# Slots of odd experts on other partitions, expert rows stored by token, and the last norm's weights spread by TensorE

## The reference, cut to what matters

```python
logits = h @ w_router + b_router                 # 320 x 32
top_v, top_e = lax.top_k(logits, 4)              # four of 32 experts for each token
gate = softmax(top_v)
# for each chosen expert e of a token:
gu = xe @ w_gu[e] + b_gu[e]                      # 1024 x 2048, 8 MB of weights
gt, up = split(gu, 2)                            # clamped to 7
act = gt * sigmoid(1.702 * gt) * (up + 1.0)
out = act @ w_dn[e] + b_dn[e]                    # 1024 x 1024, 4 MB of weights
y[token] += gate * out
x = x + y
y_prompt, y_sample = rmsnorm(x, norm_final)      # for the 256 and the 64 tokens
```

## Time and profile before

| what | us |
|---|---|
| median of 3 runs | 1360.23 |
| lowest and highest | 1358.46, 1360.65 |
| the profiled execution's own time | 1357.94 |
| its span, first to last instruction | 1356.2 |
| TensorE busy | 1264.1 (93%) |
| VectorE busy | 459.0 (34%) |
| ScalarE busy | 230.7 (17%) |
| GpSimd busy | 123.2 (9%) |

### The profile page before, as it was taken

The page is one execution under the profiler, slowest core; times in us unless marked ns, Lnnn a source line. Parts: engine busy times, 40 slices in busy tenths (PEclk is TensorE's granted clock), DMA queues, the critical chain, the costliest instruction groups (busy, mean ns, idle before and its releaser), DMA issues.

```text
span 1356.2 us, 14399 instructions
## 1 busy us (share of the span) xinstructions
PE 1264.1 (93%) x5895; PEld 570.1 (42%) x5895; DVE 459.0 (34%) x809; ACT 230.7 (17%) x333; POOL 123.2 (9%) x164
## 2 busy tenths in 40 slices
PE   7999999999999999999999999999987778878786
PEld 5756766666543333333333333333322223222231
DVE  2897322211463322223113313222422222233226
ACT  4102432310221111111011111111211111111121
POOL 3110100000010100000000000100010000000020
PEclk9999999999999999999999999999999999999898
DMA  9715826465699999999999999999999999999994
GB/s 331 258 63 157 266 76 156 155 248 204 254 364 426 425 426 426 426 425 427 426 425 427 427 427 424 425 427 425 424 427 425 425 427 425 425 426 426 424 388 153
DMA packets 97115, 479.33 MB, mean 353 GB/s; under 512 B 43962, under 2 KB 46026, under 8 KB 72311
## 3 DMA queue, kind: packets, MB, share of 16 engines
q1 hardware_dynamic: 84641, 459.36, 83.3%
q0 software_dynamic: 11008, 15.63, 3.3%
q10 hardware_dynamic: 1374, 3.02, 0.6%
HBM read 477.57 MB, written 22.61 MB: 369 GB/s over the span
## 4 chain that ended last, share of the span: by engine, by line
PE 74%; DMA 23%; issue 1%; DVE 1%; ACT 0%; DVEq 0%; ACTq 0%
PE PS L1762 29%; PE PS L1400 15%; PE PS L1795 14%; DMA ring<-in_w_dn 12%; DMA ring<-in_w_gu 11%; PE PS L1340 4%; PE PS L1580 4%; PE PS L1624 3%; PE PS L1436 2%; PE PS L1847 1%; PE PS L1667 0%; PE PS L1527 0%; DMA XX<-in_x_prompt 0%; PE PS L1546 0%; PE PS L1644 0%
## 5 line engine op out<-in xcount | busy, mean ns | idle before, releaser
L1762 PE MATMUL PS<-ring,arena 128*64 128x512 f32 x1824 | 405.7, 597 | 39.2 <-DMA ring<-in_w_gu 27.6
L1251 DVE TENSOR_TENSOR arena<-PS,XX 128x1024 f32<-128x1024 f32 x32 | 39.2, 1224 | 659.2 <-PE PS L1762 659.2
L1762 PEld LDWEIGHTS PS<-ring,arena 128*64 128x64 f32 x1824 | 129.2, 139 | 293.7 <-issue 291.1
L1795 PE MATMUL PS<-ring,arena 128*64 128x512 f32 x896 | 203.7, 604 | 16.9 <-DMA ring<-in_w_dn 15.6
L1400 PE MATMUL PS<-arena,ring 128*128 128x320 f32 x768 | 213.5, 434 | 0.1
L1400 PEld LDWEIGHTS PS<-arena,ring 128*128 128x128 f32 x768 | 144.3, 190 | 58.7 <-issue 2.0
L1762 PE MATMUL PS<-arena 128*64 128x512 f32 x608 | 136.3, 595 | 11.6 <-DMA arena<-in_w_gu 10.8
L854 ACT ACTIVATE arena<-arena 128x1024 f32<-128x1024 f32 x32 | 33.9, 1058 | 618.4 <-DVE arena L1254 618.4
L554 POOL DMA_INDIRECT y_rows<-arena x60 | 59.8, 996 | 791.7 <-ACT arena L835 762.9
L1795 PEld LDWEIGHTS PS<-ring,arena 128*64 128x64 f32 x896 | 62.0, 139 | 142.0 <-issue 142.0
L1340 PEld LDWEIGHTS PS<-ident,arena 128*128 128x128 f32 (+3 forms) x580 | 63.1, 142 | 54.8 <-issue 49.0
(11 more groups left out here) (216 smaller groups left out, 670.2 us busy)
## 6 DMA issues: line engine op xcount, KB each, us to landing
ring<-in_w_gu SPq DMA_DIRECT2D x96, 2048.0 KB, 27.9
ring<-in_w_dn SPq DMA_DIRECT2D x48, 2048.0 KB, 29.3
arena<-in_w_gu SPq DMA_DIRECT2D x31, 2048.0 KB, 28.7
arena<-in_w_dn SPq DMA_DIRECT2D x16, 2048.0 KB, 30.0
ring<-in_w_in SPq DMA_DIRECT2D x11, 2048.0 KB, 11.3
ring<-in_w_mem_kv SPq DMA_DIRECT2D x2, 2048.0 KB, 20.7
ring<-in_cache_mem_k SPq DMA_DIRECT2D x32, 128.0 KB, 3.3
ring<-in_cache_mem_v SPq DMA_DIRECT2D x4, 1024.0 KB, 6.1
```

The source lines that it names most:

```text
L1251: nc.vector.tensor_tensor(gbuf[:], PS[:, 0:2, :], g_bias, ALU.add).then_inc(main["g_added"], 1)
L1762: last = mm(PS[64 * h:64 * h + 64, 2 * g + b, :], in_block(xT[:, k, :], b), (spare[kk] if m == BONUS else moe_ring(m, 2)[:, kk]) [:, g * D ...
L1795: last = mm(PS[64 * h:64 * h + 64, 4 + b, :], actT[:, b, j, c * BLK:(c + 1) * BLK], moe_ring(m, 4)[:, j, h * 512:(h + 1) * 512], start=c = ...
```

## The change

- **Slots.** A second table `iota_o` is made in which bit 4 of the slot is turned round (a6 xor a5 becomes its opposite). The gathered and scattered rows of odd experts lie by it, those of even experts by `iota_s`. In `listing`, three more small instructions per tile flip bit 4 of the slot number where the expert is odd, so that the one comparison with `iota_s` still serves. `hot_weights` takes `iota_o` for expert 31.
- **Rows by token.** Rank r of token t is now row `4 t + r`. All of `y_rows` is zeroed, not half. `rank_rows(tt)` loads all four ranks of one tile of tokens, as two transfers of two ranks each: pieces of 8 KB. Three places instead of four are used, and GpSimd waits for expert 29's scatters before the first of them.
- **Sum by tile.** DVE adds the four ranks of tile 0, then those of tile 1, then those of tile 2.
- **Last norm.** ACT loads the norm's weights early as two rows of 2 KB; TensorE spreads them over the partitions by two products with a row of ones, behind its last `to_tokens`, into PSUM banks 4 and 5, and DVE reads them there. The load of 512 KB at the end is gone.
- **TensorE's order at the end.** `bias_sum(2)` and `to_tokens(0, 0)` stand ahead of `down(31)`, `to_tokens(0, 1)` and `(0, 2)` between its two chunks.

```diff
-RANK_PLACES = [PLACE[-10], PLACE[-9], PLACE[-6], PLACE[-5]]
+RANK_PLACES = [PLACE[-10], PLACE[-9], PLACE[-6]]
...
-                sp.dma_start(y_rows[2 * T:4 * T, :].rearrange("(p j) c -> p (j c)", p=P).rearrange("p (n c) -> p n c", c=512),
-                             W[0].rearrange("p b t -> p (b t)")[:, None, 0:512].to_broadcast([P, 10, 512])) \
+                sp.dma_start(y_rows.rearrange("(p j) c -> p (j c)", p=P).rearrange("p (n c) -> p n c", c=512),
+                             W[0].rearrange("p b t -> p (b t)")[:, None, 0:512].to_broadcast([P, 20, 512])) \
...
-        sp.wait_ge(main["dn_done"], NE - 2)
-        sp.dma_start(normfin, a["norm_final"].partition_broadcast(P)).then_inc(fin_in, 16)
...
-        nc.gpsimd.iota(worth[:, :, :, 1], [[2 * P, TT], [-2 * T, TOPK]], base=2 * T * (TOPK - 1) - SKIP,
-                       channel_multiplier=2, allow_small_or_imprecise_dtypes=True).then_inc(consts, 1)
+        nc.gpsimd.iota(worth[:, :, :, 1], [[2 * TOPK * P, TT], [-2, TOPK]], base=2 * (TOPK - 1) - SKIP,
+                       channel_multiplier=2 * TOPK, allow_small_or_imprecise_dtypes=True).then_inc(consts, 1)
...
+                    columns = iota_o[:, 64 * a6 + 32 * a5:64 * a6 + 32 * a5 + 32] \
+                        .rearrange("p (c d e f b) -> p b c d e f", c=2, d=2, e=2, f=2)[:, odd]
+                    nc.gpsimd.iota(columns, [[2, 2], [1, 2], [8, 2], [32, 2]],
+                                   base=4 * a6 + 16 * (1 - (a6 ^ a5)) + BLK * odd,
...
-        def rank_rows(r):
-            nc.gpsimd.dma_start(yr(r)[:, 0:2, :], y_rows[r * T:r * T + 2 * P, :].rearrange("(t p) d -> p t d", p=P)) \
-                .then_inc(yr_in[r], 16)
-            nc.gpsimd.dma_start(yr(r)[0:ROWS[2], 2, :], y_rows[r * T + 2 * P:(r + 1) * T, :]).then_inc(yr_in[r], 16)
+        def rank_rows(tt):
+            r = ROWS[tt]
+            for j in range(0, TOPK, 2):
+                nc.gpsimd.dma_start(yr(tt)[0:r, j:j + 2, :], y_tokens[tt * P:tt * P + r, j:j + 2, :]).then_inc(yr_in[tt], 16)
...
-        pool.wait_ge(main["scattered"], 32 * (DIRECT[0] - 1))
+        pool.wait_ge(main["scattered"], 32 * DIRECT[0])
         rank_rows(0)
-        pool.wait_ge(main["scattered"], 32 * DIRECT[0])
         rank_rows(1)
         pool.wait_ge(main[consumed(RINGED[-6])[0]], consumed(RINGED[-6])[2])
         rank_rows(2)
-        pool.wait_ge(main["gu_done"], NE)
-        rank_rows(3)
...
+            act.dma_start(nrow[64 + 32 * h:65 + 32 * h, :], a["norm_final"][512 * h:512 * (h + 1)][None, :]).then_inc(fin_in, 16)
...
+            link(nc.vector.tensor_scalar(turn[0:r, tt, :], R8i[0:r, tt, :], 512, None, ALU.bitwise_and))
+            link(nc.vector.tensor_scalar(turn[0:r, tt, :], turn[0:r, tt, :], 16 / 512, None, ALU.mult))
             link(nc.vector.tensor_scalar(lowi[0:r, tt, :], R8i[0:r, tt, :], 511, None, ALU.bitwise_and))
+            link(nc.vector.tensor_tensor(lowi[0:r, tt, :], lowi[0:r, tt, :], turn[0:r, tt, :], ALU.bitwise_xor))
...
-            dve.wait_ge(summed, (TOPK - 1) * TT + tt + 1)
+            dve.wait_ge(summed, TOPK * (tt + 1))
...
-        for r in range(TOPK):
-            j = TOPK - 1 - r
-            dve.wait_ge(yr_in[r], 32)
-            for tt in range(TT):
-                n = ROWS[tt]
+        for tt in range(TT):
+            n = ROWS[tt]
+            dve.wait_ge(yr_in[tt], 32)
+            for r in range(TOPK):
+                j = TOPK - 1 - r
...
-        dve.wait_ge(fin_in, 16)
+        dve.wait_ge(norm_spread, 1)
...
         def amid_last():
-            bias_sum(2, False)
-            to_tokens(0, 0)
+            to_tokens(0, 1)
+            to_tokens(0, 2)
...
             pe.wait_ge(main["actT_ready"], NE)
+            bias_sum(2, False)
             pe.wait_ge(main["zs_ready"], NE - 1)
+            to_tokens(0, 0)
             down(0, e, amid_last)
-            to_tokens(0, 1)
-            to_tokens(0, 2)
...
+            spread_norm()
+
+        def spread_norm():
+            pe.wait_ge(fin_in, 32)
+            for h in range(2):
+                last = mm(PS[:, 4 + h, :], ones[64 + 32 * h:65 + 32 * h, :], nrow[64 + 32 * h:65 + 32 * h, :],
+                          start=True, stop=True)
+            last.then_inc(norm_spread, 1)
```

More of the change, by code:

```diff
@@ L222, in program @@
     iota_s = sb("iota_s", [P, WIN])
+    iota_o = sb("iota_o", [P, WIN])
+    turn = sb("turn", [P, TT, 8], I32)
     worth = sb("worth", [P, TT, TOPK, 2])
@@ L281, in program @@
         sem(s) for s in ("bdn_in", "dense_ready", "gt_done", "gt_ready", "bd_done", "bd_added"))
-    yr_in = [sem(f"yr_in{i}") for i in range(TOPK)]
-    fin_in, fin_out = sem("fin_in"), sem("fin_out")
+    yr_in = [sem(f"yr_in{tt}") for tt in range(TT)]
+    fin_in, fin_out, norm_spread = sem("fin_in"), sem("fin_out"), sem("norm_spread")
     zeroed, hot_made, w_turned, w_copied = sem("zeroed"), sem("hot_made"), sem("w_turned"), sem("w_copied")
@@ L296, in program @@
     y_rows = nc.dram_tensor("y_rows", (TOPK * T, D), F32, kind="Internal").ap()
+    y_tokens = y_rows.rearrange("(t r) d -> t r d", r=TOPK)
     y_half = y_rows.rearrange("r (h c) -> (r h) c", h=2)
@@ L334, in moe_loaded, with yr @@
         return loaded[s] if s < SLOTS else low_in[s - SLOTS]
-    def yr(r):
-        return room(RANK_PLACES[r]).rearrange("p (t n) -> p t n", t=4)[:, 0:TT, :]
-    normfin = room(RANK_PLACES[0]).rearrange("p (t n) -> p t n", t=4)[:, TT, :]
+    def yr(tt):
+        return room(RANK_PLACES[tt]).rearrange("p (r n) -> p r n", r=TOPK)
+    nrow = XN[:, 1, 512:D]
+    normfin = PS[:, 4:6, :].rearrange("p a b -> p (a b)")
     block = ctx.enter_context(nc.Block())
@@ L504, in _ @@
                     nc.gpsimd.iota(columns, [[2, 2], [1, 2], [8, 2], [32, 2]], base=4 * a6 + 16 * (a6 ^ a5) + BLK * odd,
+                                   channel_multiplier=0, allow_small_or_imprecise_dtypes=True)
+                    columns = iota_o[:, 64 * a6 + 32 * a5:64 * a6 + 32 * a5 + 32] \
+                        .rearrange("p (c d e f b) -> p b c d e f", c=2, d=2, e=2, f=2)[:, odd]
+                    nc.gpsimd.iota(columns, [[2, 2], [1, 2], [8, 2], [32, 2]],
+                                   base=4 * a6 + 16 * (1 - (a6 ^ a5)) + BLK * odd,
                                    channel_multiplier=0, allow_small_or_imprecise_dtypes=True)
@@ L1233, in hot_weights @@
                 r = ROWS[tt]
-                link(nc.vector.tensor_scalar(hotw[x][0:r, tt, :], iota_s[0:r, :], 1024.0 + 512.0 * e, R[0:r, tt, e:e + 1],
+                link(nc.vector.tensor_scalar(hotw[x][0:r, tt, :], (iota_o if e % 2 else iota_s)[0:r, :], 1024.0 + 512.0 * e, R[0:r, tt, e:e + 1],
                                              ALU.add, ALU.is_equal))
@@ L1312, in _ @@
         dve.nop()
-        for r in range(TOPK):
-            j = TOPK - 1 - r
-            dve.wait_ge(yr_in[r], 32)
-            for tt in range(TT):
-                n = ROWS[tt]
+        for tt in range(TT):
[3 more added lines that the diff above has]
+                j = TOPK - 1 - r
                 if r:
-                    dve.wait_ge(summed, (r - 1) * TT + tt + 1)
-                nc.vector.scalar_tensor_tensor(X[0:n, tt, :], yr(r)[0:n, tt, :], gates[0:n, tt, j:j + 1], X[0:n, tt, :],
+                    dve.wait_ge(summed, TOPK * tt + r)
+                nc.vector.scalar_tensor_tensor(X[0:n, tt, :], yr(tt)[0:n, r, :], gates[0:n, tt, j:j + 1], X[0:n, tt, :],
                                                ALU.mult, ALU.add).then_inc(summed, 1)
@@ L1940, in _ @@
                 over_window(2)
+                pe.wait_ge(main["zs_ready"], 3 * NE)
                 pe.nop()
@@ L1943, in _ @@
                 bias_sum(tt, True).then_inc(bd_done, 1)
+            pe.wait_ge(main["zs_ready"], 2 * NE)
+            spread_norm()
             pe.nop()
```

## The result

The changed kernel takes 1362.4 us (median; 1358.6 to 1364.8) where the kernel before took 1358.4 beside it; the ratio is 1.0021, 95% interval 1.0014 to 1.0028, or 2.9 us more. (The two medians lie 4.0 us apart, because the times of the kernel before fall into two groups, one near 1358 and one near 1360, and a median jumps between them; the ratio with its interval is the safer figure.) In the profiled executions the span is 1359.6 us against 1356.2. The forecast was 3.4 us less. The changed time lies above its range, on the side of rival 2. That rival 2 named 1362.6 is in part chance: it counted +2.4 us from a median of 1360.23, and beside the changed kernel that median was 1358.4.

The account below looks back on a forecast made before the run. DMA bytes bound the expert stage, the slowest engine the end. Balance 4.0, norm 1.2 and pieces 1.5 us land the last rows at 1333.8; after the tile sums -3.4 us remains: 1356.8 from median 1360.23, range 1355.1 to 1358.3.

Parts of the forecast that it names:

- rival 2: At the end, turning bit 4 does nothing and eight sums follow tile 1's landing: +0.6 to +2.4 us, 1362.6; chance 0.13.
- What bounds the kernel: Expert stage: DMA moves 424 to 427 GB/s throughout; at the end DVE and TensorE wait for the slowest DMA engines.
- Where the lag comes from: End of expert stage: uneven gathered and scattered rows, 220 surplus by slot bit 4, put the worst engine 6.3 us behind the mean.
- the fit with 7.2 us: Slowest engine's lag at the end: 6.3 us from counted rows beside 7.2 us from the DMA share.
- The term of 4.0 us: Turning odd experts' bit 4 balances the DMA engines, so the last rows land 4.0 us earlier.
- Longer pieces: Rank loads at the end: 8 KB instead of 4 KB pieces save 1.5 us, bounds 0 and 3.4.
- The norm: Dropping the 512 KB norm load at the end frees every DMA engine of 1.2 us.
- The sum by tile: DVE's end: eight sums (9.8 us) follow tile 1's landing at 1330.9, four (4.9 us) follow tile 2's at 1333.8.
- the forecast add at 1340.7: DVE's end: `add_products(0)` starts at 1340.7 instead of 1344.14, 3.4 us earlier.
- the two sets of reports: Late expert stage: each weight transfer's sixteen reports form two drifting sets of eight, taken as evidence for engine = partition / 8.
- TensorE's spare of 5 us: TensorE's end: its last work is done at 1338.4, needed by DVE about 3 us after 1340.7.
- The covers: Other work hides the longer zeroing (up to 16.9 us bare), the listing and the tables (up to 1.8 each): cost 0.

Follow-up runs that it names:

- bit4_only: Kernel before with only the odd experts' slot bit 4 turned; rows by rank and norm transfer kept; ratio to the kernel before 1.0005.
- after_4kb: Changed kernel with one rank per transfer in 4 KB pieces, still one wait a tile; ratio to the kernel before 1.0025.
- after_inter: Changed kernel with 4 KB single-rank transfers, a semaphore for each rank, tiles 1 and 2 issued and summed in turn; ratio to the kernel before 0.9976.
- after_021: Changed kernel with tile 2's rows issued and summed before tile 1's; ratio to the kernel before 1.0017.
- after_fifo: Changed kernel with a semaphore for each pair of ranks, sums in the order of the transfers; ratio to the kernel before 1.0008.

## Why the prediction was wrong

**What bounds the kernel**: right. 424 to 428 GB/s to 1290 us in both kernels, and the last landing is set by the slowest DMA engine.

**Where the lag comes from**: this step failed. "If a DMA engine serves eight neighbouring partitions" was an assumption; from it came 220 surplus rows, 6.3 us, and the fit with 7.2 us that made it look proved. The fit was chance. The lag has two parts, neither of them the halves by bit 4: TensorE's instruction fetches on one set of eight engines (they make most of the 8.8 us between the sets, which are 4.0 when half of the code is gone) and rows inside each set (4.9 us, 2.3 with the four low bits turned). The term of 4.0 us is 0 (bit4_only). The rule that was told against it, of the Trainium skill's page "DMA: Bandwidth & Descriptors", section "The descriptor swizzle", was right for the gathered rows, and the two sets that I held against the rule have another source.

**Longer pieces**, 1.5 us: not above 0, the lower bound; the rows end 0.5 us later with them, and the weights 7 us (after_4kb).

**The norm**, 1.2 us: 1.0 to 1.1 at the last landing.

**The sum by tile**: the mechanism of rival 2, right in kind. From the forecast add at 1340.7 to the measured 1347.6 it is 6.9 us: 4.0 of balance, 1.5 of pieces, 0.2 of norm, 0.7 because tile 2 follows tile 1 by 2.2 us and not 2.9, and 0.5 because a sum that waits for the one before it on the same tile takes 1.30 us from start to start and not the 1.22 of neighbours on different tiles (10.95/9 in the earlier trace rows, 9.80/8 in after_inter). Rival 2's own sum was +0.6 to +2.4; its terms give +2.1 for pieces that bring nothing (1340.5 - 1.2 - 2.9 + 9.8 is 1346.2), and with the last three differences +3.5, which is what the profile shows. Its chance of 0.13 was too low: what spoke against it were the two sets of reports, and these had nothing to do with the turned bit.

**TensorE's spare of 5 us**: mostly gone. Its last weights came 5.1 us later instead of 4.0 earlier, and what was left, 2.2 us, it owed to a DVE that was late itself: in after_021 and after_fifo, where DVE is through sooner, TensorE is what ends last. So the 7 us that long pieces take from the weights would cost as soon as the sums no longer do.

**The covers**: all held within 0.4 us.

**Why the fastest version is faster**: the changed kernel joins rows kept by token with a wait for a whole tile. The first costs nothing at the landings; the second takes from DVE the work that it could do while the rows arrive. after_inter keeps the layout, waits rank by rank and gains.

## What to carry to other kernels

Before a balance of DMA engines is priced, find out which engine serves what: here 4.0 of the 6.7 us by which the last rows were to land sooner hung on an assignment that no row showed. A fit between two sizes is no proof while the assignment is assumed. Behind the last transfers, count the work that can only start once each has landed: a wait for a whole tile at once (here eight sums, 10.4 us, behind one landing) costs what could have been done after its first rank, and interleaving independent accumulations makes each step shorter besides (1.20 us here instead of 1.30). And before two profiled executions are compared at their ends, compare them at the start of the stage: here five of seventeen came about 2 us late out of the mixer.

## What the runs showed of the hardware

- TensorE's instruction fetches (70 packets of 16 KB, 1.07 us each) are 0.3% of DMA time on the page, but they lie on one set of eight engines (39 of 39 placed), and the two sets drift apart by 8.8 us over some 900 us; with 23 of 52 fetches gone, by 4.0.
- A row gathered to a partition 32 further is served by the same engine: in bit4_only the distance of the two sets stays within 0.2 us, and the 51 rows gathered for expert 13, whose slots are turned there, lie three or four on each engine, as before (by eight neighbouring partitions it would be two to four). Half rows scattered by GpSimd are spread more evenly than one engine for a partition would give: 26 of them on sixteen engines, one or two each.
- Pieces of 8 KB instead of 4 KB in a queue that shares the engines with weights moved the last weights' landing from 1328.7 to 1335.6 us, and the rows' own last landing from 1339.0 to 1339.5.
- 240 one-byte memsets in a row on GpSimd cost 32 us, 0.13 us each.
